# Attention loop of a two-block layer: the small products of a step gathered into one episode on the matrix engine

## What is computed

```python
hn = rms_norm(h, norm_w)
u_f, g_f, q, k, v, g_a = split(hn @ w_in)
f = fft2(u_f, axes=(1, 3)).real ; y_f = einsum(f, w_fourier) * silu(g_f)
q = rms_norm(q, q_norm_w) * HEAD_DIM ** -0.5 ; k = rms_norm(k, k_norm_w)
for c, (window, dilation) in enumerate(((128, 1), (512, 4), (2048, 16))):
    o_c, lse_c = dilated_window_attention(q[c], k[c], v[c], window, dilation, slopes)
o = sum(softmax(lse) * o_c) ; y_a = o * silu(g_a)
h = h + concat(y_f, y_a) @ w_out
```

## Time and profile before

| | us |
|---|---|
| median of 3 runs | 1461.02 (1460.84 to 1461.31) |
| the profiled execution | 1461.31 |
| its span in the trace | 1459.5 |
| TensorE busy (PE) | 1451.3, 99% of the span |
| GpSimd, VectorE, ScalarE busy | 968.0, 850.9, 518.7 |
| granted clock of TensorE | full in all 40 slices |

### The profile page before, as it was taken

One profiled execution on the slowest core, in us unless ns is written; L12 is line 12 of the kernel. 1 busy time (PEld: TensorE's weight loads), 2 busy tenths in 40 slices (PEclk: granted clock), 3 DMA queues, 4 the chain that ended last, 5 costly groups with the idle time before them and its releaser, 6 DMA issues.

```text
span 1459.5 us, 22876 instructions
## 1 busy us (share of the span) xinstructions
PE 1451.3 (99%) x8038; PEld 1196.2 (82%) x8038; DVE 850.9 (58%) x1217; ACT 518.7 (36%) x931; POOL 968.0 (66%) x945
## 2 busy tenths in 40 slices
PE   9999999999999999999999999999999999999999
PEld 6788888888888888888988888888898888888887
DVE  3577796787688747423745545500258583846733
ACT  4481551362262311112522222200153554636441
POOL 5466767776766799888267777799426654655554
PEclk9999999999999999999999999999999999999999
DMA  9343433533533345435032232334223221222232
GB/s 378 119 128 114 161 102 130 178 110 124 185 112 121 119 137 171 139 104 200 15 101 90 97 101 96 100 121 144 87 98 116 78 82 59 86 72 72 72 130 73
DMA packets 68126, 172.31 MB, mean 118 GB/s; under 512 B 7744, under 2 KB 24512, under 8 KB 66656
## 3 DMA queue, kind: packets, MB, share of 16 engines
q1 hardware_dynamic: 45648, 150.57, 31.0%
q10 hardware_dynamic: 22416, 20.92, 4.7%
HBM read 167.20 MB, written 4.27 MB: 117 GB/s over the span
## 4 chain that ended last, share of the span: by engine, by line
PE 97%; DVE 1%; DMA 1%; ACT 0%; SPq 0%; issue 0%; DVEq 0%; ACTq 0%
PE ps L628 17%; PE ps L631 17%; PE ps L630 17%; PE ps L645 6%; PE ps L647 5%; PE ps L646 5%; PE ps L960 4%; PE ps L958 4%; PE ps L959 4%; PE ps L874 1%; PE ps L985 1%; PE ps L981 1%; PE ps L983 1%; PE ps L1155 1%; PE ps L1234 1%; PE ps L1235 1%
## 5 line engine op out<-in xcount | busy, mean ns | idle before, releaser
L578 POOL TENSOR_SCALAR w_hi<-raw 128x512 fp32r<-128x512 f32 x386 | 260.5, 693 | 462.7 <-PE ps L631 211.7
L583 POOL TENSOR_TENSOR w_lo<-raw,w_hi 128x512 fp32r<-128x512 f32 x386 | 543.6, 1429 | 0.0
L628 PE MATMUL ps<-h_hi,w_hi 128*128 128x512 f32 x880 | 344.5, 391 | 0.2
L631 PE MATMUL ps<-h_hi,w_lo 128*128 128x512 f32 x880 | 342.7, 389 | 0.0
L630 PE MATMUL ps<-h_lo,w_hi 128*128 128x512 f32 x880 | 342.5, 389 | 0.0
L628 PEld LDWEIGHTS ps<-h_hi,w_hi 128*128 128x128 f32 x880 | 165.2, 188 | 36.3 <-issue 2.4
L631 PEld LDWEIGHTS ps<-h_hi,w_lo 128*128 128x128 f32 x880 | 165.2, 188 | 34.9
L630 PEld LDWEIGHTS ps<-h_lo,w_hi 128*128 128x128 f32 x880 | 165.2, 188 | 33.7
L645 PE MATMUL ps<-h_hi,w_hi 128*128 128x512 f32 x352 | 140.2, 398 | 0.4 <-ACT qsq_hi L1653 0.4
L647 PE MATMUL ps<-h_hi,w_lo 128*128 128x512 f32 x352 | 137.4, 390 | 0.0
L646 PE MATMUL ps<-h_lo,w_hi 128*128 128x512 f32 x352 | 137.3, 390 | 0.0
(11 more groups left out here) (445 smaller groups left out, 2853.3 us busy)
## 6 DMA issues: line engine op xcount, KB each, us to landing
raw<-stream SPq DMA_DIRECT2D x231, 512.0 KB, 3.3
ada_raw<-ada SPq DMA_DIRECT2D x64, 256.0 KB, 3.3
ada<-ada_first SPq DMA_DIRECT2D x8, 1024.0 KB, 14.6
abc<-acs_dram ACTq DMA_DIRECT2D x16, 512.0 KB, 6.9
raw<-stream SPq DMA_DIRECT2D x8, 256.0 KB, 12.6
xr<-x_classes ACTq DMA_DIRECT2D x1, 2048.0 KB, 10.9
x_dram<-xr ACTq DMA_DIRECT2D x1, 2048.0 KB, 7.2
x_res<-x_dram ACTq DMA_DIRECT2D x2, 1024.0 KB, 7.7
```

What stands on the lines that cost most here:

```text
L578: nc.gpsimd.tensor_scalar(hi[:, w], raw[:, raw_slot, w], 1.0, 1.0, ALU.mult, ALU.mult).then_inc(split_hi, 1)
L583: ins = nc.gpsimd.tensor_tensor(lo[:, w], raw[:, raw_slot, w], hi[:, w].bitcast(F32), ALU.subtract)
L628: nc.tensor.matmul(ps[:, bank], hi[:, w], x_hi[:, k0 + k], start=start and k == 0, stop=False)
L631: mm = nc.tensor.matmul(ps[:, bank], lo[:, w], x_hi[:, k0 + k], start=False, stop=stop and k == tiles - 1)
```

## The change

The small products of TensorE are put in another order, and ScalarE's list follows.

- `turn_p(a, r)` moves from behind the fourth half of step r to behind its sixth (in step 3 it stays behind half 21), and `scores(a, r + 1)` follows it at once, before the next halves.
- `attend(a, r)` moves to behind the sixth half of step r + 1 (for r = 2: behind half 21), ahead of `turn_p(a, r + 1)`. `attend(a, 3)` stays. Its wait on `biased` goes.
- The turns of the values leave `follow` (except for pair 0, ahead of the loop) and become `turn_v`, behind `scores(a, 3)`, behind `turn_p(a, 3)`, and ahead of `attend(a, 3)`. `vT` gets three buffers, 4 KB more.
- On ScalarE both `pt_out` of step r move to the head of step r + 1 (in step 3 behind `take` of unit 10), `take_v` is split from `take`, and in step 0 `take` of unit 1 now comes ahead of `hi_fourier` and of the copy into `wf_now`.
- VectorE's list isn't changed.

```diff
-        vT = g("vT", [P, S])
+        vT = g("vT", [P, CFG, S])
@@ TensorE
-                if 7 <= j <= 9:
-                    c = j - 7
-                    pe.wait_ge(evacuated, E_ATT + N_ATT * p + 6 + c + 1)
-                    ...
+                if 7 <= j <= 9 and is_first(p):
+                    turn_v(p, j - 7)
+
+            def turn_v(p, c):
+                pe.wait_ge(evacuated, E_ATT + N_ATT * p + 6 + c + 1)
+                if c:
+                    pe.wait_ge(v_ready, 3 * p + c)
+                else:
+                    pe.wait_ge(qk_root, 6 * p + 6)
+                for t in range(NT):
+                    mm = nc.tensor.transpose(ps[:, 7, t * P:(t + 1) * P], vT[:, c, t * P:(t + 1) * P], ident)
+                mm.then_inc(v_turned, 1)
             def attend(a, r):
                 pe.wait_ge(pt_ready, 1 + 16 * a + 4 * r + 4)
-                if r < NT - 1:
-                    pe.wait_ge(biased, 1 + 8 * a + 2 * (r + 1))
@@
-                for r in range(NT):
-                    scores(a, r)
-                    if r == 0:
-                        token_transform(a)
-                    half(a + 1, 6 * r)
-                    half(a + 1, 6 * r + 1)
-                    half(a + 1, 6 * r + 2)
-                    half(a + 1, 6 * r + 3)
-                    turn_p(a, r, 0)
-                    turn_p(a, r, 1)
-                    if r == NT - 1:
-                        transform_heads(a + 1)
-                    half(a + 1, 6 * r + 4)
-                    half(a + 1, 6 * r + 5)
-                    attend(a, r)
+                scores(a, 0)
+                token_transform(a)
+                for x in range(0, 6):
+                    half(a + 1, x)
+                turn_p(a, 0, 0)
+                turn_p(a, 0, 1)
+                scores(a, 1)
+                for x in range(6, 12):
+                    half(a + 1, x)
+                attend(a, 0)
+                turn_p(a, 1, 0)
+                turn_p(a, 1, 1)
+                scores(a, 2)
+                for x in range(12, 18):
+                    half(a + 1, x)
+                attend(a, 1)
+                turn_p(a, 2, 0)
+                turn_p(a, 2, 1)
+                scores(a, 3)
+                turn_v(a + 1, 0)
+                for x in range(18, 22):
+                    half(a + 1, x)
+                attend(a, 2)
+                turn_p(a, 3, 0)
+                turn_p(a, 3, 1)
+                turn_v(a + 1, 1)
+                transform_heads(a + 1)
+                for x in range(22, 24):
+                    half(a + 1, x)
+                turn_v(a + 1, 2)
+                attend(a, 3)
                 attend_near(a)
@@ ScalarE
                 for r in range(NT):
+                    if r:
+                        pt_out(a, r - 1, 0)
+                        pt_out(a, r - 1, 1)
+                    if r == NT - 1:
+                        take_v(a + 1, 0)
                     exp(a, r, 0)
                     exp(a, r, 1)
                     scale_bias(r)
                     if r == 0:
                         take_odd(a)
                     take(a + 1, 3 * r)
-                    pt_out(a, r, 0)
+                    take(a + 1, 3 * r + 1)
                     if r == 0:
                         hi_fourier(a)
                         act.wait_ge(fv_done, a + 1)
                         A(wf_now[:], blocks(wf, a + 1), ACT.Copy).then_inc(wf_ready, 1)
-                    take(a + 1, 3 * r + 1)
-                    pt_out(a, r, 1)
                     if r == NT - 1:
+                        pt_out(a, r, 0)
+                        pt_out(a, r, 1)
+                        take_v(a + 1, 1)
                         take_heads(a + 1)
                     take(a + 1, 3 * r + 2)
+                take_v(a + 1, 2)
                 hi_attention(a)
                 move_v(a + 1)
```

More of the change, by code:

```diff
@@ L1654, in take @@
                 elif j < 9:
-                    if not (first and j == 6):
-                        act.wait_ge(v_turned, 3 * p + j - 6)
+                    if not first:
+                        act.wait_ge(v_turned, 3 * p - 2 + j - 6)
                     if j == 6:
-                        A(natural(vT[:]), permuted(bank), ACT.Copy).then_inc(evacuated, 1)
+                        A(natural(vT[:, 0]), permuted(bank), ACT.Copy).then_inc(evacuated, 1)
                     else:
-                        A(vT[:], bank, ACT.Copy).then_inc(evacuated, 1)
+                        A(vT[:, j - 6], bank, ACT.Copy).then_inc(evacuated, 1)
                 elif j == 9:
@@ L1680, in take, with take_v @@
                       scale=1.0 if m < 3 else 1.0 / HP).then_inc(qk_root, 1)
[L1681 to L1686, removed]
+                if 7 <= j <= 9 and first:
+                    take_v(p, j - 7)
+            def take_v(p, c):
+                act.wait_ge(v_turned, 3 * p + c + 1)
+                if c == 0 and not is_first(p):
+                    act.wait_ge(v_moved, 3 * p)
+                A(vN_next[:, c], ps[:, 7].rearrange("p (t w) -> p t w", t=NT), ACT.Copy).then_inc(v_ready, 1)
             def take_heads(p):
```

## The result

The changed kernel takes 1463.65 us (median of 20 runs, 1463.45 to 1466.06), the kernel before, beside it, 1461.46 (20 runs). The ratio is 1.0017 with an interval of 1.0011 to 1.0023: 2.2 us slower, and within 0.2%. The profiled execution has a span of 1462.1 us where it was 1459.5, at a full granted clock.

A forecast was written before the change was run, and what follows sets the result against it. TensorE, busy to the end of each 85.57 us iteration, was taken to bound the kernel. Product order +0.65 and the wait +1.5 gave +2.15 on a median of 1461.02: 1463.2 us, eight-in-ten range 1461.2 to 1466.4.

The forecast's parts named there:

- Step 1, the order of products: TensorE's small products in the loop: 18 changes of shape instead of 15, +0.22 us an iteration, +0.65 in all.
- the load in the open of a turn behind another shape: TensorE, from `attend` or `scores` to a turn: uncovered weight load, taken as 0.06 us, between almost nothing and 0.11.
- the credit for the four returns that fell away: TensorE's returns to long products: three from a turn save 0.05 us each, one from `scores` becoming `scores` to turn saves 0.08.
- Step 3, the wait: TensorE ahead of L1082 in step 0 waits for `split_squares` behind later `hi_fourier`: 0.5 us an iteration, +1.5 in all.
- Step 4, the rest: Other moves, such as `pt_out`, `take_v` of the last turn and step 3's copies, cost 0 while they stay covered.
- The Fourier chain meets GpSimd: VectorE's two subtractions run at disturbed length beside GpSimd: +5.4 us, 1466.4; chance 0.23.
- The wait doesn't show: ScalarE and VectorE chain 0.33 us shorter, only the order of products counts: +0.65, 1461.7 us; chance 0.15.
- Episodes cost by their number: Entering and leaving long products is the price, not shapes: -2.6 us, 1459.9 with the wait, 1458.4 without; chance 0.05.

The follow-up runs named there:

- the first experiment: Changed kernel with `hi_fourier` put back ahead of `take` of unit 1 on ScalarE in step 0: 1462.21 us, ratio 1.0006.
- the cut of `attend`: Changed kernel with each of the first three `attend` cut in two, half ahead of the turns and half behind: 1465.53 us, ratio 1.0032.
- the kernel with both corrections: Changed kernel with `hi_fourier` back ahead of `take` of unit 1 and the turns ahead of `attend` in the joined episodes: 1461.13 us, ratio 0.9999.
- the kernel with its `attend` last: Kernel before, nine episodes and old ScalarE list, with the four `attend` of a pair moved to the loop's end: 1460.40 us, ratio 0.9992.
- the kernel with the longer chain: Changed kernel with the bias scaling and the copy into `wf_now` ahead of `hi_fourier` in step 0, ending it 0.7 us later: 1469.02 us.

## Why the prediction was right

**The time.** Forecast 1463.2, that is +2.15; measured 1463.65, +2.2 over the runs of before beside it, which themselves read 1461.46 instead of the 1461.02 that I started from. That the sum comes so close is partly luck. The two terms were 0.22 and 0.50 us an iteration and measured 0.38 and 0.44, so their errors partly cancel: 0.72 forecast, 0.82 measured, or 2.4 to 2.5 us for the loop where the medians differ by 2.2.

**Step 1, the order of products.** Forecast +0.22 an iteration, bounds 0.05 and 0.37; measured 0.38 by the first experiment, 0.01 above the upper bound. The mechanism held each time it was tried: three changes fewer are -0.40 (forecast -0.42), the cut of `attend` is +0.59 (forecast +0.57). The term that I had to bound, the load in the open of a turn behind another shape, came out as taken: eight turns with a drain behind them last 1.02 in the step's episode, 0.87 + 0.09 + 0.06, and from the first turn to the second it is 0.17 (1182.42 to 1182.58) where the next follow at 0.11.

The term that was mis-sized is the credit for the four returns that fell away, three of them put at 0.05 each. It shows when the starts in the second iteration are summed for the small and for the 300 long products, before and in the kernel of the first experiment, which has no wait. The small ones take 16.13 and 16.89: +0.76, and the terms of the forecast that fall on them make +0.75 (three changes 0.45, three last turns no longer cut short 0.24, one load behind the scores 0.06). The long ones take 69.40 and 69.03: -0.37, where four returns at 0.13 to 0.14 were to give -0.53. The five returns that remain cost more each than the nine did (0.15 against 0.12 on average, with a pace of 0.2267), and those 0.16 are the whole distance from 0.22 to 0.38. The kernel with both corrections says the same: four episodes fewer, all with a return from a turn, should have given back 4 x 0.05 = 0.20 and gave 0.03 to 0.09.

**Step 3, the wait.** Forecast 0.5 an iteration, by a chain over three engines; measured 0.44. Every station can be checked, with 0.16 to be taken off, by which the loop of the profiled execution starts later: ScalarE 1155.53 (forecast 1155.53), `hi_fourier` 1159.00 (1159.00), `yo_lo` 1159.79 (1159.80), `qsq_lo` 1160.40 (1160.42), L1082 1161.14 against 1161.11 plus 0.06.

**Step 4, the rest.** No other wait of TensorE appears in the loop. `take_v` of the last turn and the copies of step 3 stayed covered.

**The rivals.** *The Fourier chain meets GpSimd* didn't happen but is real: the chain that was 0.7 us longer ran into it with one of its two subtractions, which took 1.10. *The wait doesn't show* is excluded by the row of the waits. *Episodes cost by their number* is refuted as an explanation of the change, by the order swapped inside unchanged episodes. It is not worth nothing: four episodes fewer gave 0.03 to 0.09 us in one pair of kernels and 0.23 to 0.25 in another.

## What to carry to other kernels

Small products are cheap beside long ones as long as they have the same tile shape; count the changes of shape before moving them, put those of the long products' shape at the edge of an episode, and gather those of one other shape, here at the price of three small buffers. When a step leaves an engine's list, look at what was parked behind its wait: here the rounding that VectorE's queue waited for (`hi_fourier`) stood there, right behind the copy of the turned probabilities. That copy left, the next unit's work with its table load was put ahead, and the rounding came 2.4 us later, although that work could start 1.1 sooner. A margin between two engines is read from both sides, and a shortened list on the waiting side eats it as surely as a longer one on the other.

## What the runs showed of the hardware

- Going from long products to turns of the same shape adds nothing (0.23 to the next start, as between long ones); going to another shape 0.09, and the first weight load is then in the open, 0.05 for 128 x 64, 0.06 for a turn, 0.11 for a long product's. The trace agrees with the rule of the Trainium skill's page "TensorEngine Tiling (Array Packing)", section "Key Properties", that a change of the tiling mode drains.
- The long products behind an episode are not at their pace at once: several follow at 0.23 to 0.24 instead of 0.227, and how much that adds isn't constant. It is 0.13 to 0.14 behind `attend` and scores and 0.17 to 0.18 behind scores alone when before is set beside the kernel with its `attend` last. But what stood in the episode doesn't decide it alone: in the kernel with both corrections the 48 long products behind one and the same episode of step 2 take 0.04 more in the first iteration than in the second. Why isn't shown; nothing was tried on it.
- A subtraction of 128 x 512 on VectorE took 0.68 us with GpSimd pausing, and 1.10 to 1.64 beside it: the rest of GpSimd's instruction and then 0.54.
- The profiled execution of the kernel with the longer chain is 1.6 us late when its loop begins (1145.66 against 1144.04 for the first product), although nothing is changed ahead of the loop. The granted clock of its first 100 us is 0.98, where it is 1.00 before and after the change. Its runs lie in two groups, 1467.1 to 1467.4 and 1469.0 to 1469.4; the first is what the loop explains (1463.65 + 3 x 1.18 = 1467.2). The mean granted clock of the two runs in the first group is 1.000 and of the three in the second 0.999. The same goes for the other kernels: the single runs that lie 1.8 to 2.4 us above their median (1463.39 of before, 1466.06 of the change, 1464.57 with the turns ahead of `attend`, 1467.62 with `attend` cut) have 0.999, and all other runs 1.000. So some 2 us more go with a lower granted clock, and in the one such execution that was profiled it fell at the start; what lowers it isn't shown.
